# Stick-breaking attention: one head's half of the turned probabilities is copied by VectorE, the other by ScalarE

## The chip, the cores and the metric

The kernel runs on one core of a Trainium2 chip. The metric is the time of one execution on the device in microseconds (us). The core's engines work side by side, each through its own queue in order: TensorE (PE in the profile, with its weight loads as PEld), VectorE (DVE), ScalarE (ACT), GpSimd (POOL) and SyncE (SP), which issues the weight DMAs. They wait for one another through semaphores only.

## What is computed

The program is a whole small model: two blocks of a first network (sparse attention with retention, then stick-breaking attention, each with a convolutional feed-forward part) and one block of a second network. The change lies in the stick-breaking attention, for 16 heads of width 64 over 528 tokens:

```python
def stick_breaking(q, k, v):
    """Strictly causal stick-breaking attention over 128-query blocks. (B,L,H,d) -> (B,L,H,d)."""
    ...
        z = jnp.einsum('bqhd,bkhd->bhqk', q[:, s:e], k[:, :e]).astype(jnp.float32) * scale
        mask = (jnp.arange(e)[None, :] < jnp.arange(s, e)[:, None])[None, None]
        log_1m = jnp.where(mask, jax.nn.log_sigmoid(-z), 0.0)
        rest = lax.cumsum(log_1m, axis=3, reverse=True) - log_1m
        a = jnp.where(mask, jnp.exp(jax.nn.log_sigmoid(z) + rest), 0.0)
        outs.append(jnp.einsum('bhqk,bkhd->bqhd', a.astype(v.dtype), v[:, :e]))
```

The kernel works with products in place of sums of logarithms: a = sigmoid(z) times the running product of sigmoid(-z).

## The kernel before

The order of all work is written out by hand, engine by engine; each stage has one function for each engine. For the stick-breaking stage these are stick_pe, stick_act and stick_dve. The heads are taken in 8 pairs; the 528 queries of a pair are cut into three steps of different width, so there are 24 steps. Step n belongs to pair b = n // 3 and has position x = n % 3. Position 0 has 432 columns a head (three scans a head, of 272, 144 and 16 columns), position 1 has 400, position 2 has 528.

A step passes through these stations:
- stick_z (L1640), TensorE: scores of both heads into two neighbouring PSUM banks, one a head, bank Z_BANK[n % 2] and the next. Signal z_made.
- sigmoids (L1743, L1746), ScalarE: sigmoid(z) into keep, sigmoid(-z) into rest. Signal s_made.
- scans (L1796), VectorE: the running products in rest, head 0, then head 1. Then the multiplication keep times rest (L1807), which makes the probabilities a. Signal a_made.
- stick_turn (L1653, L1656), TensorE: 128x128 blocks of a are turned. Four blocks a head go back into the two banks of the scores (each head has its own bank of 512 columns), odd ones into another bank. Signal a_turned.
- copies (L1762 for the odd blocks, into AX, at two of three positions; L1763 for the 2 x 512 columns of both heads, into AT), ScalarE. Signal a_copied.
- stick_av (L1675), TensorE: product of V with the turned probabilities, into one sum for the pair. It waits for a_copied of its step, and at position 0 also for oT_lo, which says that the pair before has been taken out of PSUM. Signal o_used.
- the pair's result is split into a high part (L1751 on ScalarE, all but four columns; L1754 for those four) and a low part (L1799 and L1803 on VectorE, signals oT_lo and lead_lo).

The stations of different steps are interleaved. In iteration n, TensorE does: filling work, stick_turn of step n-1, filling work, stick_av of step n-1, stick_z of step n+1. The filling work are matmul groups of the projections of later pairs, and at the end of the output projection (L346): four to six groups an iteration up to n = 20, one or two after that, four in n = 24. One projection unit is eight groups; its sum uses one PSUM place, so the next unit starts only when VectorE has taken out the last one (stick_evac, L365 and L367).

ScalarE in iteration n: the sigmoids of step n, a part of a pair's result, then the copies L1762 and L1763 of step n-1, and at positions 0 and 1 (up to pair 7 and pair 6) the split of a weight unit into its high part (L431), after which GpSimd makes the low part (L2574).

VectorE in iteration n: stick_evac at positions 1 and 2 (up to n = 20), the scans of step n, a low part of a result, the multiplication L1807 of step n. It has no copy of turned blocks.

Of the kernel before, what the change touches and what calls it, by code (L numbers as in the profile page):

```python
# [9 lines left out]
ACT = mybir.ActivationFunctionType  # L10
# [155 lines left out]
def program(nc, xT, w_all, params, consts, extra, sinks, relb1, relb2, scratch, out):  # L166
    ctx = ExitStack()
    with ctx:
# [9 lines left out]
        ps = ctx.enter_context(nc.psum_tensor("ps", [P, 8, 512], F32))  # L178
# [43 lines left out]
        class Cut:  # L222
# [39 lines left out]
            "m_std", "mg_sum", "mg_hi", "memset_done", "stage_dve", "o_used", "row_done", "gain_both", "rs_first",  # L262
            "rs_mean", "rs_second", "gate_act", "row_bias", "out_gate", "u_made", "u_read", "mo_exp", "m_sq",
            "e_read", "m_h", "m_hi", "m_y", "m_lo", "ret_t", "ret_sum", "ret_sq", "ret_hi", "ret_y", "ret_lo",
            "mo_den", "mo_done", "m_den", "m_rd", "a_made", "lead_lo", "a_turned", "a_copied", "s_made", "lead_hi",
            "sink_neg", "sel_made", "part_hi", "part_rest", "part_mid", "part_lo")}
        turn_done = [signal(f"turn_done{q}") for q in range(2)]
        turn_out = [signal(f"turn_out{q}") for q in range(2)]
# [1291 lines left out]
        STEPS = 3 * PAIRS  # L1560
# [98 lines left out]
        def stick_av(pe, d, m):  # L1659

            b, x = m // 3, m % 3
            pe.wait_ge(sig["a_copied"].sem, m + 1)
            if x == 0 and b:
                pe.wait_ge(sig["oT_lo"].sem, b)
            for t, tiles in STEP_AV[x]:
                c0, c1 = (0, LEAD) if t < 0 else (LEAD + P * t, LEAD + P * t + P)
                for i, (s, slot) in enumerate(tiles):
                    for hh in range(2):
                        if slot == "e0":
                            a = d["AX"][:, P * hh:P * hh + P]  # L1670
                        elif slot == "e1":
                            a = d["AX"][:, 256 + 124 * hh:256 + 124 * hh + LEAD]
                        else:
                            a = d["AT"][:, hh, P * slot:P * slot + P]
                        mm = pe.matmul(o_sums(slice(64 * hh, 64 * hh + 64), c0, c1),  # L1675
                                       d["V"][:, s, P * b + 64 * hh:P * b + 64 * hh + 64], a,
                                       start=(i == 0), stop=(i == len(tiles) - 1), skip_group_check=True)
            sig["o_used"].by(mm)
# [47 lines left out]
        def stick_act(act):  # L1726
# [8 lines left out]
            for n in range(STEPS + 2):  # L1735
# [19 lines left out]
                if 0 <= n - 1 < STEPS:  # L1755
                    m, bank = n - 1, Z_BANK[(n - 1) % 2]
                    act.wait_ge(sig["a_turned"].sem, m + 1)
                    if m:
                        act.wait_ge(sig["o_used"].sem, m)
                    e = EXTRA_COLS[m % 3]  # L1760
                    if e:
                        act.activation(d["AX"][:, 0:e], ps[:, A_BANK, 0:e], ACT.Copy)  # L1762
                    sig["a_copied"].by(act.activation(d["AT"], ps[:, bank:bank + 2, :], ACT.Copy))  # L1763
                if x == 1 and b + 1 < PAIRS:
                    split_after(act, CQK, (2 * b + 2,))
                if x == 0 and 1 <= b < PAIRS:
# [2 lines left out]
        def stick_evac(v, u):  # L1769
            q_k = stick_qk(u // 2)[u % 2]  # L1770
            woven_evac(v, CQK.first + u, UB, q_k[:, ::-1] if u % 2 else q_k, 1.0 if u % 2 else 64 ** -0.5)

        def stick_dve(v):
            d = stick_views()
# [11 lines left out]
            for n in range(STEPS + 2):  # L1786
# [3 lines left out]
                if n < STEPS:  # L1790
                    w, keep, rest = STEP_WIDTH[x], d["keep"][x], d["rest"][x]
                    v.wait_ge(sig["s_made"].sem, n + 1)
                    for hh in range(2):
                        for at, k, first in STEP_SCANS[x]:
                            r = rest[:, hh * w + at:hh * w + at + k]
                            dve.by(v.tensor_tensor_scan(r, r, d["start"][:, first:first + k], 0.0, ALU.mult, ALU.add))  # L1796
                if x == 1 and n >= 4:
                    v.wait_ge(sig["oT_hi"].sem, b)
                    sig["oT_lo"].by(v.tensor_tensor(rest_cols(Yl, b - 1), o_sums(slice(0, P), LEAD, T3),  # L1799
# [1014 lines left out]
```

## Time and profile before

| what | us |
|---|---|
| median of 3 runs | 2392.09 |
| lowest and highest run | 2391.22, 2392.62 |
| the profiled execution | 2387.57 |
| its span in the profile | 2385.80 |
| TensorE busy | 2348.3 (98%) |
| VectorE busy | 1103.0 (46%) |
| ScalarE busy | 854.6 (36%) |
| GpSimd busy | 919.2 (39%) |

The stick-breaking steps lie between 918 and 1100 us from the start of the span. Times of the profile are counted from there. A row of the timeline names the start, the duration, the engine, the line, the operation and its operands, how many follow one another, and in brackets the idle time of the engine just before, with the instruction that ended it. All of the kernel's arena is in SBUF, ps is PSUM. The granted clock of TensorE was 1.00 throughout the stage.

### The profile page before, as it was taken

The page shows a single profiled execution, that of the slowest core. Times are in us where ns is not written, and L with a number is a line of the kernel's source. Part 1 is how long each engine was busy: PE and PEld are TensorE (multiplying, and loading weights), DVE is VectorE, ACT ScalarE, POOL GpSimd, SP SyncE. Part 2 cuts the span into 40 slices and gives each one's busy share as a digit, 9 for nine tenths or more (in the row PEclk, how much of TensorE's full clock was granted, in tenths as well). Part 3 has the DMA queues.
Part 4 walks back from the last instruction along what each step waited for, and adds up shares of the span by engine and source line. Part 5 has one row for each costly group of instructions (what it writes and reads, how often), then busy time and mean ns, then how long its engine had stood idle before and what let it go on. Part 6 is the DMA issues. An engine that isn't in the chain of part 4 may idle for free.

```text
span 2385.8 us, 37842 instructions
## 1 busy us (share of the span) xinstructions
PE 2348.3 (98%) x15316; PEld 2066.7 (87%) x15316; DVE 1103.0 (46%) x1676; ACT 854.6 (36%) x1320; POOL 919.2 (39%) x382
## 2 busy tenths in 40 slices
PE   7999999999999999999999999999999999999999
PEld 7898999999999999898988888767667888888887
DVE  4885353573442534555644435343473337422222
ACT  4334433332222334554322224454464333322222
POOL 4321223344444442123444444422224455444443
PEclk9999999999999999999999999999999999999999
DMA  5121222222222231111232222322213333323232
GB/s 179 66 72 37 73 65 87 89 88 93 87 103 88 88 107 59 54 54 54 89 105 88 90 104 89 107 72 71 71 54 106 106 106 106 106 88 105 88 106 88
DMA packets 33463, 208.12 MB, mean 87 GB/s; under 512 B 3754, under 2 KB 6420, under 8 KB 9284
## 3 DMA queue, kind: packets, MB, share of 16 engines
q1 hardware_dynamic: 29552, 202.00, 24.7%
q10 hardware_dynamic: 3796, 4.45, 0.6%
q8 instruction: 89, 1.46, 0.3%
q14 instruction: 26, 0.21, 0.0%
HBM read 204.24 MB, written 2.12 MB: 86 GB/s over the span
## 4 chain that ended last, share of the span: by engine, by line
issue 59%; POOL 24%; PE 16%; POOLq 1%; DMA 0%; ACT 0%; DVE 0%; SPq 0%; DVEq 0%; ACTq 0%
POOL wl L2574 24%; PE ps L393 14%; PE ps L346 1%; PE ps L328 1%; POOLq L2573 0%; POOLq L2578 0%; DMA raw<-in_w_all 0%; ACT L431 0%; ACT wh L431 0%; PE ps L489 0%; DVE X L464 0%; SPq L2541 0%; DVEq L464 0%; ACTq L430 0%
## 5 line engine op out<-in xcount | busy, mean ns | idle before, releaser
L2574 POOL TENSOR_TENSOR wl<-raw,wh 128x1024 fp32r<-128x1024 f32 x376 | 918.9, 2448 | 1450.0 <-ACT wh L431 1449.8
L431 ACT ACTIVATE wh<-raw 128x1024 fp32r<-128x1024 f32 x376 | 395.2, 1054 | 758.3 <-PE ps L393 501.5
L393 PE MATMUL ps<-Hh,wl 128*128 128x264 f32 (+2 forms) x1736 | 480.6, 325 | 0.0
L393 PE MATMUL ps<-Hl,wh 128*128 128x264 f32 (+2 forms) x1736 | 480.6, 325 | 0.0
L393 PE MATMUL ps<-Hh,wh 128*128 128x264 f32 (+2 forms) x1736 | 480.5, 325 | 0.0
L393 PEld LDWEIGHTS ps<-Hh,wh 128*128 128x128 f32 x1736 | 291.7, 188 | 28.5 <-issue 0.2
L393 PEld LDWEIGHTS ps<-Hh,wl 128*128 128x128 f32 x1736 | 291.1, 188 | 27.8
L393 PEld LDWEIGHTS ps<-Hl,wh 128*128 128x128 f32 x1736 | 291.1, 188 | 27.4
L346 PE MATMUL ps<-Hh,wh 128*128 128x264 f32 (+1 forms) x1056 | 277.4, 326 | 4.9 <-DVE arena L365 4.0
L346 PE MATMUL ps<-Hl,wh 128*128 128x264 f32 (+1 forms) x1056 | 255.9, 306 | 0.0
L346 PE MATMUL ps<-Hh,wl 128*128 128x264 f32 (+1 forms) x1056 | 255.8, 306 | 0.0
L393 PE MATMUL ps<-Yh,wh 128*128 128x512 f32 (+1 forms) x844 | 251.4, 338 | 0.7 <-DVE Yl L888 0.7
L393 PE MATMUL ps<-Yl,wh 128*128 128x512 f32 (+1 forms) x844 | 251.3, 338 | 0.0
L393 PE MATMUL ps<-Yh,wl 128*128 128x512 f32 (+1 forms) x844 | 251.2, 338 | 0.0
L464 DVE TENSOR_TENSOR X<-ps,X 128x512 f32 (+4 forms) x96 | 67.0, 697 | 328.0 <-PE ps L393 289.9
L346 PEld LDWEIGHTS ps<-Hh,wh 128*128 128x128 f32 x1056 | 171.0, 188 | 43.3 <-issue 31.6
L346 PEld LDWEIGHTS ps<-Hl,wh 128*128 128x128 f32 x1056 | 171.0, 188 | 9.6 <-issue 2.4
L346 PEld LDWEIGHTS ps<-Hh,wl 128*128 128x128 f32 x1056 | 170.8, 188 | 9.6
L393 PEld LDWEIGHTS ps<-Yh,wh 128*128 128x128 f32 x844 | 145.0, 188 | 17.6 <-DVE Yl L888 0.9
L393 PEld LDWEIGHTS ps<-Yl,wh 128*128 128x128 f32 x844 | 144.8, 188 | 16.7
L393 PEld LDWEIGHTS ps<-Yh,wl 128*128 128x128 f32 x844 | 144.7, 188 | 16.7
L642 DVE SCALAR_TENSOR_TENSOR arena<-arena,par 128x528 f32<-128x528 f32 (+1 forms) x44 | 106.9, 2430 | 7.3 <-DVE arena L640 4.1
(255 smaller groups left out, 2810.8 us busy)
## 6 DMA issues: line engine op xcount, KB each, us to landing
raw<-in_w_all SPq DMA_DIRECT2D x188, 1024.0 KB, 4.8
X<-in_xT SPq DMA_DIRECT2D x4, 528.0 KB, 9.3
arena<-scratch ACTq DMA_DIRECT2D x2, 1024.0 KB
arena<-in_extra ACTq DMA_DIRECT2D x2, 528.0 KB
out<-X SPq DMA_DIRECT2D x1, 1024.0 KB, 4.2
out<-X SPq DMA_DIRECT2D x4, 256.0 KB, 2.0
arena<-in_extra ACTq DMA_DIRECT2D x2, 264.0 KB
cst<-in_consts SPq DMA_DIRECT2D x1, 448.0 KB, 11.1
```

Source lines behind the costliest of these rows:

```text
L328: mm = pe.matmul(ps[:, 2 * j + h, 0:c1 - c0], w[:, j, k, :], moving(x, k, c0, c1), start=(k == 0 and part == 0), stop=(k == KB - 1 and par ...
L346: mm = pe.matmul(ps[:, bank + h, 0:c1 - c0], w[:, j, k, :], moving(x_, blk, c0, c1), start=(first and part == 0), stop=(last and part == 2))
L393: mm = pe.matmul(ps[:, 2 * j + h + bank, 0:c1 - c0], w[:, j, k, :], moving(x, blk, c0, c1), start=(at == 0 and part == 0), stop=(at == len ...
L431: act.activation(wh[:, j], raw[:, j // 2, :, P * (j % 2):P * (j % 2) + P], ACT.Copy).then_inc(hi_split, 1)
L464: v.tensor_tensor(x, acc(j, T), x, ALU.add).then_inc(acc_free[j], 1)
L642: dve.by(v.scalar_tensor_tensor(out=c1[:, mm], in0=gs[:, mm, skip + 1:T + 1], scalar=w[mm][1], in1=c1[:, mm], op0=ALU.mult, op1=ALU.add))
L2574: pool.tensor_tensor(wl[:, j], raw[:, j // 2, :, P * (j % 2):P * (j % 2) + P], wh[:, j].bitcast(F32), ALU.subtract).then_inc(split_ready[j ...
```

## The change

ScalarE's copy L1763 takes only head 0 (512 columns of the first bank). Head 1's half, the second bank, is copied by VectorE in a new helper half_copy, with a signal a_half of its own. In iteration n, VectorE does it for step n-1 between the scans of head 0 and the scans of head 1 of step n; for the last step it stands alone in iteration 24. stick_av waits for both signals. half_copy waits for a_turned of its step and for o_used of the one before, the same two for which ScalarE's copy waits.

```diff
@@ stick_av
             pe.wait_ge(sig["a_copied"].sem, m + 1)
+            pe.wait_ge(sig["a_half"].sem, m + 1)
@@ stick_act
-                    sig["a_copied"].by(act.activation(d["AT"], ps[:, bank:bank + 2, :], ACT.Copy))
+                    sig["a_copied"].by(act.activation(d["AT"][:, 0], ps[:, bank, :], ACT.Copy))
@@ new, before stick_dve
+        def half_copy(v, d, m):
+            v.wait_ge(sig["a_turned"].sem, m + 1)
+            if m:
+                v.wait_ge(sig["o_used"].sem, m)
+            sig["a_half"].by(v.tensor_copy(d["AT"][:, 1], ps[:, Z_BANK[m % 2] + 1, :]))
@@ stick_dve, in the loop over n
                     for hh in range(2):
                         for at, k, first in STEP_SCANS[x]:
                             r = rest[:, hh * w + at:hh * w + at + k]
                             dve.by(v.tensor_tensor_scan(r, r, d["start"][:, first:first + k], 0.0, ALU.mult, ALU.add))
+                        if n and hh == 0:
+                            half_copy(v, d, n - 1)
+                if n == STEPS:
+                    half_copy(v, d, n - 1)
```

VectorE's queue in the order of the program, from the scans of a step at position 2 to the scans of the next step at position 0. Before (a scan is printed there as SCALAR_TENSOR_TENSOR):

```order
L1796 SCALAR_TENSOR_TENSOR arena<-arena 128x528 x2
L1803 TENSOR_TENSOR Yl<-ps,Yh 128x4
L1807 TENSOR_TENSOR arena<-arena 128x1056
L1796 SCALAR_TENSOR_TENSOR arena<-arena 128x272
L1796 SCALAR_TENSOR_TENSOR arena<-arena 128x144
L1796 SCALAR_TENSOR_TENSOR arena<-arena 128x16
L1796 SCALAR_TENSOR_TENSOR arena<-arena 128x272
L1796 SCALAR_TENSOR_TENSOR arena<-arena 128x144
L1796 SCALAR_TENSOR_TENSOR arena<-arena 128x16
L1807 TENSOR_TENSOR arena<-arena 128x864
```

After, the same place (L1803 is now the scan, L1814 and L1818 are the old L1803 and L1807):

```order
L1803 SCALAR_TENSOR_TENSOR arena<-arena 128x528
L1778 COPY arena<-ps 128x512
L1803 SCALAR_TENSOR_TENSOR arena<-arena 128x528
L1814 TENSOR_TENSOR Yl<-ps,Yh 128x4
L1818 TENSOR_TENSOR arena<-arena 128x1056
L1803 SCALAR_TENSOR_TENSOR arena<-arena 128x272
L1803 SCALAR_TENSOR_TENSOR arena<-arena 128x144
L1803 SCALAR_TENSOR_TENSOR arena<-arena 128x16
L1778 COPY arena<-ps 128x512
L1803 SCALAR_TENSOR_TENSOR arena<-arena 128x272
L1803 SCALAR_TENSOR_TENSOR arena<-arena 128x144
L1803 SCALAR_TENSOR_TENSOR arena<-arena 128x16
```

A copy stands between the heads of each step, so head 1's scans and the multiplication come behind it.

TensorE's queue at the first product with V, with the semaphores that it waits for. Before:

```order
L346 MATMUL ps<-Hh,wh 128x264 x2
L346 MATMUL ps<-Hl,wh 128x264 x2
L346 MATMUL ps<-Hh,wl 128x264 x2
L1675 MATMUL ps<-arena 64x128 [waits a_copied]
L1675 MATMUL ps<-arena 64x128 x9
```

After:

```order
L346 MATMUL ps<-Hh,wh 128x264 x2
L346 MATMUL ps<-Hl,wh 128x264 x2
L346 MATMUL ps<-Hh,wl 128x264 x2
L1676 MATMUL ps<-arena 64x128 [waits a_half,a_copied]
L1676 MATMUL ps<-arena 64x128 x9
```

Nothing changes place on TensorE; one wait is added to each product.

## Rows read from the trace of the kernel before

**Rows 1.** Busy us by stretch: PE, PEld, DVE, ACT, POOL, then clock, DMA.
```profile
967.00:1075.00 108.00, 107.80 (x1013) 97.02 (x1013) 55.45 (x80) 54.86 (x82) 24.05 (x10) 1.00 0.15 50
1075.00:1093.00 18.00, 14.61 (x149) 12.53 (x146) 9.60 (x16) 10.46 (x16) 2.92 (x1) 1.00 0.00 1
```

**Rows 2.** Groups by form: line, engine, operation, shape, count | busy us, mean ns.
```profile
L1763 ACT ACTIVATE arena<-ps 128x1024 f32<-128x1024 f32 x24 | 24.6, 1025 | 13.8 <-PE ps L1656 13.8
...
L735 ACT ACTIVATE arena<-ps 128x512 f32<-128x512 f32 x4 | 2.4, 600 | 4.7 <-PE ps L695 4.7
...
L1796 DVE TENSOR_TENSOR_SCAN arena<-arena 128x528 f32<-128x528 f32 x16 | 19.2, 1241 | 3.7 <-ACT arena L1743 3.7
...
L737 DVE TENSOR_SCALAR arena<-ps 128x512 f32<-128x512 f32 x6 | 4.2, 692 | 7.5 <-PE ps L695 7.5
...
L1141 DVE COPY arena<-ps 64x528 f32<-64x528 f32 x1 | 0.7, 711 | 2.7 <-PE ps L1031 2.7
```

**Rows 3.** Timeline (start, us, what), a regular iteration at position 2.
```profile
959.05 2.40 DVE L1796 TENSOR_TENSOR_SCAN arena<-arena 128x528 f32<-128x528 f32 x2
...
960.90 0.86 PEld L1675 LDWEIGHTS ps<-arena 128*64 128x64 f32 x16
```

**Rows 4.** Timeline, a regular iteration at position 0 and the next turning.
```profile
942.33 2.21 DVE L1796 TENSOR_TENSOR_SCAN arena<-arena 128x272 f32<-128x272 f32 x6 [2.05 <-ACT arena L1743]
...
943.64 1.02 ACT L1763 ACTIVATE arena<-ps 128x1024 f32<-128x1024 f32 x1
...
944.57 1.06 DVE L1807 TENSOR_TENSOR arena<-arena 128x864 f32<-128x864 f32 x1
...
944.71 1.08 PEld L1675 LDWEIGHTS ps<-arena 128*64 128x64 f32 x20
...
945.68 2.37 POOL L2574 TENSOR_TENSOR wl<-raw,wh 128x1024 fp32r<-128x1024 f32 x1 [13.32 <-ACT wh L431]
...
948.41 0.47 PEld L1653 LDWEIGHTS ps<-cst,arena 128*128 128x128 f32 x4
...
950.03 0.49 ACT L1762 ACTIVATE arena<-ps 128x384 f32<-128x384 f32 x1 [0.70 <-PE ps L1656]
```

**Rows 5.** Timeline, the last iterations n = 21, 22 and 23, by engine.
```profile
1077.24 2.21 DVE L1796 TENSOR_TENSOR_SCAN arena<-arena 128x272 f32<-128x272 f32 x6 [2.15 <-ACT arena L1743]
1083.04 1.88 DVE L1796 TENSOR_TENSOR_SCAN arena<-arena 128x400 f32<-128x400 f32 x2 [2.50 <-ACT arena L1746]
1084.83 0.67 DVE L1799 TENSOR_TENSOR Yl<-ps,Yh 128x512 fp32r<-128x512 f32 x1
1090.10 2.41 DVE L1796 TENSOR_TENSOR_SCAN arena<-arena 128x528 f32<-128x528 f32 x2 [3.71 <-ACT arena L1743]
...
1079.85 2.92 POOL L2574 TENSOR_TENSOR wl<-raw,wh 128x1024 fp32r<-128x1024 f32 x1 [12.61 <-ACT wh L431]
...
1078.88 1.09 PEld L1675 LDWEIGHTS ps<-arena 128*64 128x64 f32 x20 [0.88 <-ACT arena L1763]
...
1081.86 0.46 PEld L1653 LDWEIGHTS ps<-cst,arena 128*128 128x128 f32 x4
...
1085.61 1.32 PEld L1675 LDWEIGHTS ps<-arena 128*64 128x64 f32 x24 [1.66 <-ACT arena L1763]
...
1091.10 0.86 PEld L1675 LDWEIGHTS ps<-arena 128*64 128x64 f32 x16 [1.47 <-ACT arena L1763]
```

**Rows 6.** Timeline, two places elsewhere where VectorE and GpSimd overlap.
```profile
456.99 2.29 DVE L548 SCALAR_TENSOR_TENSOR Hl<-X,par,Hh 128x528 fp32r<-128x528 f32 x1
459.20 2.90 DVE L554 TENSOR_TENSOR arena<-arena 128x528 f32<-128x528 f32 x1
...
458.87 2.66 POOL L2574 TENSOR_TENSOR wl<-raw,wh 128x1024 fp32r<-128x1024 f32 x1 [0.16 <-ACT wh L431]
...
1571.06 2.36 POOL L2574 TENSOR_TENSOR wl<-raw,wh 128x1024 fp32r<-128x1024 f32 x1 [15.56 <-ACT wh L431]
...
1571.49 3.01 DVE L2114 TENSOR_TENSOR_SCAN arena<-arena 4x512 f32<-4x512 f32 x1
```

More of the change, by code:

```diff
@@ L264, in program @@
             "e_read", "m_h", "m_hi", "m_y", "m_lo", "ret_t", "ret_sum", "ret_sq", "ret_hi", "ret_y", "ret_lo",
-            "mo_den", "mo_done", "m_den", "m_rd", "a_made", "lead_lo", "a_turned", "a_copied", "s_made", "lead_hi",
+            "mo_den", "mo_done", "m_den", "m_rd", "a_made", "lead_lo", "a_turned", "a_copied", "a_half", "s_made", "lead_hi",
             "sink_neg", "sel_made", "part_hi", "part_rest", "part_mid", "part_lo")}
```

## The prediction

> **What bounds the kernel now.** I read first the busy time by stretch, to see whether TensorE has any room in the stick-breaking stage, then TensorE's weight loads in order of time, to see what its few gaps wait for, and last the same seconds on VectorE, ScalarE and GpSimd. TensorE is the bound: in the regular part of the stage it is busy 107.80 of 108.00 us, so a copy made shorter on another engine gives nothing there. In the last steps it is busy 14.61 of 18.00 us, because the filling work has thinned out to one group of matmuls at a time [rows 1]. There it waits three times before the product with V (L1675): 0.88 us, 1.66 us and 1.47 us [rows 5]. The profile puts all three on ScalarE's copy L1763. The first and the third are that: step 20's copy starts long after the turned blocks are there, and the product follows its end. The second is not: this product also needs the low part of the pair before, L1799 on VectorE, which starts at 1084.83, takes 0.67 and ends at 1085.50; the product starts at 1085.61. So from VectorE's end to TensorE's start I count 0.11 us.
>
> **What one half costs on either engine.** ScalarE's copy falls from 128x1024, 1.025 us, to 128x512; the nearest row is L735 with 0.600 us [rows 2]. So ScalarE is free 0.43 us earlier, 24 times. VectorE gets 24 copies of 128x512 out of PSUM. The nearest rows are L737, a TENSOR_SCALAR of that shape from PSUM, 0.692 us, and L1141, a real COPY from PSUM, 0.711 us for 528 columns and 64 partitions; I take 0.69 us. Bounds are 0.60 (as fast as ScalarE) and 0.71. Two instructions in a row on VectorE overlap by some 0.08: two scans of 1.241 us take 2.40 together, a stride of 1.16. So what follows a copy is moved by about 0.61, I take 0.60.
> The Trainium skill (VectorE: DVE Perf Modes, section on the TRN2 errata) prices a copy from PSUM on VectorE at 120 cycles plus one a column at 0.96 GHz, an estimate of 0.66 us for 512 columns. By it every term below in which the copy's end counts would be 0.03 smaller, 0.2 in the whole sum; the measured rows decide.
>
> **The regular steps.** A step has position x = n mod 3. *x = 2* (seven steps, n = 2 to 20): the scan of head 0 starts at 959.05, the copy can start 1.16 later at 960.21, ends at 960.90, and TensorE can go on at 961.01. Before, the product started at 960.90 [rows 3]. That is 0.11 us later, for the six steps n = 2 to 17. The seventh, n = 20, I leave out: its filling work is already the output projection's, with a start of its own. **Six times 0.11 = 0.66 us.** With a copy of 0.60 it would be near 0.1, with 0.71 it is 0.8.
> *x = 0*: the scans start at 942.33; two heads and the start of the multiplication lie 2.24 apart, so one head takes about 1.08. The copy runs from 943.41 to 944.10 and TensorE may start at 944.21; it starts at 944.71 anyway. Nothing lost. The multiplication L1807 moves from 944.57 to 945.17 and would end at 946.23; the turning that needs it starts at 948.41 [rows 4]. Nothing lost either, unless GpSimd gets in between (a rival below).
> *x = 1*: ScalarE shows the turned blocks ready at 950.03 [rows 4]; the copy is done within 1 us of that, and four groups of filling matmuls stand between the turning and the product, so it is hidden. The evacuations L365 and L367, on which TensorE's next unit waits, stand ahead of the scans in VectorE's order and are not touched. The extra wait on TensorE I take at nothing: products with one and with two waits start alike.
>
> **The last steps**, where nothing hides a wait [rows 5].
> *n = 21 (x = 0)*, product of step 20: scans start at 1077.24, the copy at 1078.32, it ends at 1079.01; TensorE goes on at 1079.11 where it did at 1078.88: **+0.23**. ScalarE's half is ready 0.4 earlier, but now VectorE's comes last.
> Then GpSimd. ScalarE's weight split stands right behind its copy and moves 0.43 earlier, and with it GpSimd's L2574, from 1079.85 to 1079.42. VectorE's scans of head 1 have been moved to 1078.92 to 1080.08 and stand in the way. What happens then, other places show [rows 6]: GpSimd's instruction came at 458.87 while VectorE ran L548; as L548 ended, at 459.28, GpSimd went first, and VectorE's next instruction took 2.90 us, until 0.57 after GpSimd's end. A scan does the same: it took 3.01 us beside GpSimd's 2.36. So I expect that GpSimd takes over when the scan of 272 columns ends (1079.64) and runs about 2.25 us, to 1081.89; the rest of the scans ends near 1082.2, the multiplication runs from 1082.31 to 1083.37, and the turning of step 21 starts at 1083.48. Without GpSimd it would start at 1081.86 + 0.23 = 1082.09.
> *n = 22 (x = 1)*: the turned blocks are there 1.62 later (948.41 to 950.03 in [rows 4]), at 1085.10. VectorE, done with head 0's scan by 1084.2, stands waiting for them; copy to 1085.79, head 1's scan from 1085.70, L1799 from 1086.59 to 1087.26, product at 1087.37 where it was 1085.61: **+1.76 in all so far** (0.23 + 0.60 = 0.83 if GpSimd did not come in between: the copy alone moves L1799 by 0.60).
> *n = 23 (x = 2)*: the scans start at 1090.10 after ScalarE, so they only move with the rest. Copy from 1091.26 to 1091.95, product at 1092.06 instead of 1091.10: **+0.96**. The last copy (n = 24) has four groups to hide behind.
> Sum for the last steps: 1.76 + 0.96 = **2.72 us**; with 0.66 from the regular steps **3.4 us longer**. It adds to TensorE's stream, which has no gap behind the stage that could take it up. The profiled execution took 2387.57 us (span 2385.80), 4.5 under the median of the runs, 2392.09; the 3.4 us are the same in both. **Forecast: 2395.5 us**, plus 0.14%.
>
> **The rivals.**
> *A. GpSimd does not get in between in n = 21.* Then the last steps cost 0.23 + 0.60 + 0.96 = 1.79 and the whole 2.45: 2394.5 us. For it: no row shows a takeover between two scans of one run, and they follow each other without a gap. Against it: the takeover at 458.87 was between two instructions without a gap as well. Chance 0.25.
> The Trainium skill (SBUF — State Buffer, section on who interferes with whom) says that VectorE's instructions with two SBUF inputs and GpSimd's that read SBUF exclude each other for a whole instruction, and that a VectorE instruction with at most one SBUF input does not contend. The rows on L554 and the scan agree; by the same rule the added copy, which reads PSUM, is itself never held up, and B and C below hang on the moved instructions alone.
> *B. Slower by more than 0.2%: GpSimd gets in ahead of the multiplication in the regular x = 0 steps.* GpSimd's split moves from 945.68 to 945.25, the multiplication from 944.57 to 945.17 [rows 4]: VectorE is ahead by 0.08, where it was ahead by 1.1. If the copy or its wait costs 0.1 more than I take, GpSimd goes first, to 947.62; the multiplication (0.57 behind it for 0.70 us, so 0.93 for its 1.06) ends at 948.55, and the turning starts at 948.66 instead of 948.41. That is 0.25 for each of six steps, 1.5 us: 2397.0 us, just past the 0.2%. It decides from 0.1 us on, and both moved times are estimates; but the copy's 0.69 is well shown and its blocks are ready in time. Chance 0.2.
> *C. Faster, or no loss: the halves really run side by side.* If VectorE's half were ready with ScalarE's, the products at 1078.88 and 1091.10 would come 0.4 earlier each, and 2391.3 us is the least I can reach. Against it: VectorE's scans start after ScalarE's sigmoids in every step, and the copy stands behind one head of them; in n = 23 ScalarE's own copy would be done before VectorE's starts. Chance 0.05. A gain over 0.2% would need 4.8 us, more than all three waits together.
>
> **How the numbers follow.** Forecast 0.5, A 0.25, B 0.2, C 0.05. A measurement of this kernel tells 0.2%, 4.8 us, from no change. The forecast, A and C are within it; B lies on its edge, and a stall that I have missed would come on top. So faster 0.03, same 0.77, slower 0.20. The range takes in A with a copy of 0.60 us and half of C below, 2392.0, and above B with a copy of 0.71 us and 1 us for what the waits themselves cost, 2398.5.
>
> **What would show it.** In the profile after: 24 rows of COPY from PSUM near 0.69 us, 24 of ScalarE's copy near 0.60; in the regular x = 2 steps a product that starts 0.1 later behind VectorE's copy; in the last steps TensorE waiting for VectorE at three products, with about 2.7 us more idle time between 1075 and 1096, and a scan or multiplication on VectorE of over 2 us at n = 21. Wrong it would be if that scan is not held up (A), if L1807's successor in regular x = 0 steps takes 3 us (B), if the copies take over 0.8 us or wait for the turned blocks in every step, or if TensorE shows new gaps at the evacuations.

## The result, and the profile after

| | before | changed |
|---|---|---|
| median, us | 2390.85 (2387.92 to 2392.71, 22 runs) | 2395.08 (2391.25 to 2396.05, 22 runs) |
| the profiled execution, us | 2387.57 | 2391.54 |
| its span, us | 2385.8 | 2389.7 |

The changed kernel takes 1.0016 times as long, with an interval of 1.0010 to 1.0022: about 3.8 us more (2.4 to 5.3). The 0.2% that were set as the bound of "no change" are 4.8 us; the ratio is within it, and only the upper end of its interval is past it. The medians themselves are 4.2 us apart, the lowest runs 3.3. Forecast were 3.4 us more and 2395.5 us. The two profiled executions are 3.97 us apart.

The 22 times of either kernel stand in two clusters: before, 9 at 2387.9 to 2388.5, 11 at 2391.2 to 2392.7 and 2 between; changed, 5 at 2391.3 to 2391.7 and 17 at 2393.9 to 2396.1. The profiled execution of either kernel lies at its lower cluster. One execution of a later kernel (regular steps only) took 6447.61 us and is left out of that kernel's ratio.

The busy time by stretch stands first, as in [rows 1]. Columns are the stretch, its length, busy us of PE, PEld, DVE, ACT and POOL with the number of instructions, then granted clock and DMA share.

```profile
967.00:1075.00 108.00, 107.58 (x1005) 96.90 (x1005) 73.25 (x95) 49.25 (x82) 27.93 (x10) 1.00 0.14 50
1075.00:1093.00 18.00, 14.17 (x141) 11.83 (x136) 12.05 (x17) 8.77 (x16) 2.35 (x1) 1.00 0.00 1
1094.00:1100.00 6.00, 5.11 (x37) 4.81 (x38) 3.20 (x5) 0.00 (x0) 0.00 (x0) 0.72 0.00 0
```

In the regular part TensorE is still busy nearly throughout. VectorE has grown from 55.45 to 73.25 us and ScalarE has shrunk from 54.86 to 49.25, and neither matters to TensorE there. VectorE's growth is more than its 15 added instructions: about half of it is a wait, shown below at position 1. The last line is new: a granted clock of 0.72 over 6 us in the last steps, where it was 1.00 before. 6 x 0.28 = 1.7 us of TensorE's time is lost at half clock (1.2 GHz in place of 2.4).

The two halves, groups by form, answer to [rows 2]:

```profile
L1778 DVE COPY arena<-ps 128x512 f32<-128x512 f32 x24 | 16.1, 670 | 4.5 <-PE ps L1656 4.5
L1764 ACT ACTIVATE arena<-ps 128x512 f32<-128x512 f32 x24 | 14.3, 596 | 13.7 <-PE ps L1656 13.7
```

A regular iteration at position 2, VectorE and then TensorE's weight load, answers to [rows 3]:

```profile
959.72 1.25 DVE L1803 TENSOR_TENSOR_SCAN arena<-arena 128x528 f32<-128x528 f32 x1
960.88 0.67 DVE L1778 COPY arena<-ps 128x512 f32<-128x512 f32 x1
...
961.66 0.89 PEld L1676 LDWEIGHTS ps<-arena 128*64 128x64 f32 x16 [0.24 <-issue]
```

The copy ends at 961.55 and the product starts 0.11 later, 1.94 us behind the first scan where it was 1.85 before. A regular iteration at position 0 answers to [rows 4]:

```profile
943.00 1.16 DVE L1803 TENSOR_TENSOR_SCAN arena<-arena 128x272 f32<-128x272 f32 x3 [1.58 <-ACT arena L1744]
944.08 0.67 DVE L1778 COPY arena<-ps 128x512 f32<-128x512 f32 x1
...
945.84 1.06 DVE L1818 TENSOR_TENSOR arena<-arena 128x864 f32<-128x864 f32 x1
...
945.92 3.21 POOL L2585 TENSOR_TENSOR wl<-raw,wh 128x1024 fp32r<-128x1024 f32 x1 [12.80 <-ACT wh L431]
```

The multiplication is 0.08 us ahead of GpSimd, as worked out, and keeps its 1.06 us; GpSimd pays, with 3.21 in place of 2.37, and nobody waits for it. One position on, at position 1, VectorE and GpSimd:

```profile
952.98 2.96 DVE L1818 TENSOR_TENSOR arena<-arena 128x800 f32<-128x800 f32 x1
...
952.71 2.37 POOL L2585 TENSOR_TENSOR wl<-raw,wh 128x1024 fp32r<-128x1024 f32 x1 [3.58 <-ACT wh L431]
```

and VectorE in the kernel before:

```profile
951.71 0.98 DVE L1807 TENSOR_TENSOR arena<-arena 128x800 f32<-128x800 f32 x1
```

In the changed kernel GpSimd is 0.27 us ahead, and the multiplication takes 2.96 us where it took 0.98 before. The same stands in each of the six regular steps at position 1. The prediction looked at position 0 only. It costs TensorE nothing: the multiplication ends at 955.94, and the turning that needs it starts at 958.79.

The last iterations answer to [rows 5]; VectorE, GpSimd, then TensorE's weight loads:

```profile
1078.47 1.16 DVE L1803 TENSOR_TENSOR_SCAN arena<-arena 128x272 f32<-128x272 f32 x3 [1.57 <-ACT arena L1744]
1079.54 0.67 DVE L1778 COPY arena<-ps 128x512 f32<-128x512 f32 x1
1080.12 3.28 DVE L1803 TENSOR_TENSOR_SCAN arena<-arena 128x272 f32<-128x272 f32 x3
1083.44 1.06 DVE L1818 TENSOR_TENSOR arena<-arena 128x864 f32<-128x864 f32 x1
...
1086.12 0.69 DVE L1778 COPY arena<-ps 128x512 f32<-128x512 f32 x1 [0.63 <-PE ps L1656]
...
1087.63 0.67 DVE L1810 TENSOR_TENSOR Yl<-ps,Yh 128x512 fp32r<-128x512 f32 x1
...
1094.08 0.67 DVE L1778 COPY arena<-ps 128x512 f32<-128x512 f32 x1
...
1080.66 2.35 POOL L2585 TENSOR_TENSOR wl<-raw,wh 128x1024 fp32r<-128x1024 f32 x1 [12.70 <-ACT wh L431]
...
1080.32 1.11 PEld L1676 LDWEIGHTS ps<-arena 128*64 128x64 f32 x20 [1.09 <-ACT arena L1764]
1084.56 0.42 PEld L1653 LDWEIGHTS ps<-cst,arena 128*128 128x128 f32 x4 [1.18 <-DVE arena L1818]
1088.41 1.33 PEld L1676 LDWEIGHTS ps<-arena 128*64 128x64 f32 x24 [1.81 <-issue]
1094.86 1.34 PEld L1676 LDWEIGHTS ps<-arena 128*64 128x64 f32 x16 [2.42 <-issue]
...
1103.79 1.09 PEld L1676 LDWEIGHTS ps<-arena 128*64 128x64 f32 x20
```

This is the forecast of n = 21: GpSimd comes in at 1080.66, between the scans of head 1, which take 3.28 us in place of 1.16. The multiplication is late, and TensorE gets a wait it did not have (1.18 us before the turning, L1653). At 1094.86 the weight loads of a product take 1.34 us where the same 16 took 0.86 before: that is the half clock.

Two of the brackets say "issue", and the first names ScalarE's copy, although VectorE's ended last (1080.21, and 0.11 later TensorE). With two semaphores to wait for, the bracket says little; the end of the last of the awaited instructions says it.

**Where the time went.** A distance between two products with V is free of whatever shifted the kernel earlier. The product of step n - 1 stands in iteration n. In us, from the starts of L1675 (before) and L1676 (after):

| from one product to the next | before | changed | more |
|---|---|---|---|
| a whole pair in the regular part (three steps) | 22.47 | 22.58 | 0.11, for six pairs 0.67 |
| step 19 to 20 | 5.54 | 5.76 | 0.22 |
| step 20 to 21 | 6.73 | 8.09 | 1.36 |
| step 21 to 22 | 5.49 | 6.45 | 0.96 |
| step 22 to 23 | 7.37 | 8.93 | 1.56 |

Together 4.8 us in the stage. The first four lines, 3.2 us, are the forecast's terms; the last is the clock, which it did not have. In front of the stage the changed kernel's profile is 0.5 us late already (first weight load of L793 that waits: 25.44 before, 25.89 after). Behind the stage it gets time back: before had half clock near 1575 us, in the second network, and after had not.

```profile
1572.00:1578.00 6.00, 6.00 (x21) 4.41 (x20) 3.08 (x2) 3.34 (x3) 3.07 (x2) 0.72 0.53 175
```

That is before; the changed kernel has 1.00 at this place. So the difference of the two profiled executions, 3.97, is not the forecast's sum come true: it is 3.2 of it, 1.6 of clock more and about as much less elsewhere, 0.5 of start-up, and some 0.3 that none of these account for. How much of that belongs to the change and how much to the execution is what the experiments had to tell.

### The profile page after: what moved, and what is told of

It reads as the page before. It is cut to its first block, busy times and chain, and to the rows that moved or that the text cites. A ratio compares the mean times of both kernels' runs of the same rounds, so it can differ in the third digit from the quotient of the medians.

```text
span 2389.7 us, 37906 instructions
## 1 busy us (share of the span) xinstructions
PE 2349.2 (98%) x15316; PEld 2067.2 (87%) x15316; DVE 1132.3 (47%) x1700; ACT 845.0 (35%) x1320; POOL 925.1 (39%) x382
## 3 DMA queue, kind: packets, MB, share of 16 engines
HBM read 204.24 MB, written 2.12 MB: 86 GB/s over the span
## 4 chain that ended last, share of the span: by engine, by line
issue 59%; POOL 24%; PE 16%; POOLq 1%; DMA 0%; ACT 0%; DVE 0%; SPq 0%; DVEq 0%; ACTq 0%
POOL wl L2585 24%; PE ps L393 14%; PE ps L346 1%; PE ps L328 1%; POOLq L2584 0%; POOLq L2589 0%; DMA raw<-in_w_all 0%; ACT L431 0%; ACT wh L431 0%; PE ps L489 0%; DVE X L464 0%; SPq L2552 0%; DVEq L464 0%; ACTq L430 0%
## 5 line engine op out<-in xcount | busy, mean ns | idle before, releaser
L431 ACT ACTIVATE wh<-raw 128x1024 fp32r<-128x1024 f32 x376 | 395.4, 1055 | 756.2 <-PE ps L393 498.8
```

The costliest lines, as they stand in the source:

```text
L431: act.activation(wh[:, j], raw[:, j // 2, :, P * (j % 2):P * (j % 2) + P], ACT.Copy).then_inc(hi_split, 1)
```

## The experiments

The theory was that the sum of the forecast is right and that the rest is a property of the execution, the clock falling behind the longer waits. The rival was that the change costs something else too, for instance the second wait on TensorE or the moved multiplications. So the kernels are read by the distance table, and the timing decides only where it can. All their lines are moved against the changed kernel's by one to four.

**Each of the two once more.** No edit: one more profile of the kernel before and of the changed one.

> The kernel before, unchanged, for a second trace of it. TensorE's product of step 22 at the same distance from the scans of step 23 as in the first trace (1.00 us), three waits of 0.9, 1.7 and 1.5 us in the last steps and full clock there. If the lower clock after the stage (near 1573 us in the first trace) belongs to the kernel, it is there again; if it comes and goes, it is not.

> The changed kernel, unchanged, for a second trace. Theory 1 (the waits in the last steps lower the clock): the wait before the product of step 22 is again about 2.4 us, and TensorE again runs at half clock for 3.4 us right behind it, which costs about 1.6 us. Theory 2 (the clock falls at some place of its own choosing): the half clock is elsewhere or nowhere, and the last steps cost 1.6 us less than in the first trace. The regular steps lose 0.11 us a pair by both.

The distances came back to within 0.02 us: 22.47, 5.54, 6.72, 5.50, 7.36 for the kernel before and 22.58, 5.78, 8.08, 6.45, 8.95 for the changed one. The fall of the clock in the last steps was there again in the changed kernel,

```profile
1090.00:1102.00 12.00, 9.79 (x77) 8.47 (x73) 4.77 (x6) 2.97 (x6) 0.00 (x0) 0.86 0.00 0
```

and the one near 1575 us was absent again. The kernel before had it twice as long there (12 x 0.28 = 3.4 us lost), and another one near 188 us.

```profile
188.00:192.00 4.00, 3.50 (x18) 3.53 (x19) 2.07 (x9) 1.12 (x4) 0.00 (x0) 0.59 0.82 266
1572.00:1584.00 12.00, 10.18 (x30) 7.75 (x31) 5.15 (x5) 5.26 (x7) 4.75 (x2) 0.72 0.25 87
```

So the distances belong to the kernel, and half clock comes and goes in units of 1.7 us between executions of one kernel. The two executions of the kernel before lost 1.7 and 5.1 us to it, which is 3.4 of the 3.7 us between their times. That the spread of its other runs (2387.92 to 2392.71) has the same cause is likely and not shown.

**The halves in the last steps only, and in the regular steps only.** Both start from the changed kernel. For the last steps only:

```diff
@@ stick_av
-            pe.wait_ge(sig["a_half"].sem, m + 1)
+            if m >= 20:
+                pe.wait_ge(sig["a_half"].sem, m - 19)
@@ stick_act
+                    if m >= 20:
                         sig["a_copied"].by(act.activation(d["AT"][:, 0], ps[:, bank, :], ACT.Copy))
+                    else:
+                        sig["a_copied"].by(act.activation(d["AT"], ps[:, bank:bank + 2, :], ACT.Copy))
@@ stick_dve
-                        if n and hh == 0:
+                        if n > 20 and hh == 0:
```

> Halves only for steps 20 to 23, ScalarE's full copy for the 20 steps before. My theory: the regular steps lose nothing, the last ones 2.5 to 2.9 us by waits (0.2 + 1.3 + 1.0), and about 1.6 more if the clock falls there. The rival, that the loss is spread over all steps: most of the 3.4 us is gone.

The other kernel, regular steps only, has `m < 20` for both conditions, the wait on a_half against m + 1, and half_copy for n = 1 to 20 only.

> Halves only for steps 0 to 19, ScalarE's full copy for steps 20 to 23. My theory: 0.11 us for each of six pairs, 0.7 us in all, no takeover by GpSimd at the end, the last steps as before. The rival: more than 1.5 us, if the copies cost TensorE something in every step.

| | regular pair | 19 to 20 | 20 to 21 | 21 to 22 | 22 to 23 | median | ratio |
|---|---|---|---|---|---|---|---|
| last steps only | 22.47 | 5.75 | 8.08 | 6.46 | 8.89 | 2393.75 | 1.0014 (1.0004 to 1.0024) |
| regular steps only | 22.58 | 5.55 | 6.73 | 5.49 | 7.37 | 2390.73 | 1.0001 (0.9992 to 1.0011) |

The parts are the changed kernel's to 0.04 us and do not touch one another. Last steps alone are slower by a margin that the timing can tell; the regular steps' 0.67 us it cannot. TensorE waits for a second semaphore 20 times in the second kernel and only the 0.11 a pair shows, which is the copy's end at position 2. The second wait as such costs nothing that can be seen.

**GpSimd's share in n = 21.** The last weight split before GpSimd's work (L431, at x = 0 of the last pair) is put behind the stage:

```diff
@@ stick_act
-                if x == 0 and 1 <= b < PAIRS:
+                if x == 0 and 1 <= b < PAIRS - 1:
                     ...
+                if n == STEPS:
+                    split_after(act, CQK, (2 * PAIRS - 1,))
```

> The changed kernel, but ScalarE's last weight split of the stage (unit 15, in n = 21) stands behind its copies of n = 24, so GpSimd has no work while VectorE does steps 21 and 22. If GpSimd's takeover caused part of the loss: head 1's scans in n = 21 take 1.16 us instead of 3.28, no wait before the turning of step 21, and the product of step 21 starts 0.75 to 0.9 us earlier against that of step 20. If the copy alone did it, nothing changes. If it is the amount of waiting that lowers the clock, the half clock may go as well, another 1.6 us; if only the last wait of 2.4 us counts, it stays.

VectorE and TensorE's weight loads of that kernel:

```profile
1082.69 1.15 DVE L1805 TENSOR_TENSOR_SCAN arena<-arena 128x272 f32<-128x272 f32 x3
...
1085.89 0.47 PEld L1653 LDWEIGHTS ps<-cst,arena 128*128 128x128 f32 x4
...
1090.23 2.45 PEld L1676 LDWEIGHTS ps<-arena 128*64 128x64 f32 x24 [2.25 <-issue]
```

The scans of head 1 take 1.15 again, the turning no longer waits, and step 20 to 21 falls from 8.09 to 7.34: GpSimd's share is 0.75 us, and the copy's own 0.61 remain (7.34 - 6.73). But the clock fell earlier, at this product (24 loads in 2.45 us, not 1.33), and 21 to 22 took 8.05, then 22 to 23 only 7.40. The time, 2393.53 us, is 1.0011 (1.0002 to 1.0021) times that of before. So taking away GpSimd takes away its 0.75, but in this execution not the fall of the clock. The 1.6 us of the clock (8.05 - 6.45) came one product earlier instead, behind a wait of 2.25 us.

**The copy of step 22 back on ScalarE.**

```diff
@@ stick_av
-            pe.wait_ge(sig["a_half"].sem, m + 1)
+            if m != 22:
+                pe.wait_ge(sig["a_half"].sem, m + 1 - (m > 22))
@@ stick_act
+                    if m != 22:
                         sig["a_copied"].by(act.activation(d["AT"][:, 0], ps[:, bank, :], ACT.Copy))
+                    else:
+                        sig["a_copied"].by(act.activation(d["AT"], ps[:, bank:bank + 2, :], ACT.Copy))
@@ stick_dve
-                        if n and hh == 0:
+                        if n and n != 23 and hh == 0:
```

> The changed kernel, but the copy of step 22 is ScalarE's alone, as before; 23 halves are left. The product of step 22 should start 0.96 us earlier against the scans of step 23. If the long wait there lowers the clock, the half clock goes too and the last steps are 2.5 us shorter in all; if the waits of n = 21 and 22 do it, only 0.96.

```profile
1091.58 1.32 PEld L1677 LDWEIGHTS ps<-arena 128*64 128x64 f32 x24 [1.81 <-issue]
1097.07 0.86 PEld L1677 LDWEIGHTS ps<-arena 128*64 128x64 f32 x16 [1.47 <-ACT arena L1768]
```

21 to 22 is back at 5.49, 22 to 23 at 7.37, and the wait is the 1.47 of [rows 5] again. The clock stayed at 1.00 in the last steps; this is one trace, and the kernels below keep 1.00 there with the long wait too, so it does not show that the shorter wait is the reason. The 0.96 are this one copy, as forecast. Median 2390.84, ratio 1.0004 (0.9995 to 1.0014).

**Is GpSimd ahead of the multiplication (rival B)?** In the changed kernel the margin is 0.08 us. A fill of unused columns ahead of the multiplication uses it up:

```diff
@@ stick_dve, ahead of the multiplication
+                if x == 0 and 0 < n < 21:
+                    v.memset(arena[:, 13000:13192], 0.0)
```

> The changed kernel with one memset of 192 unused columns (about 0.2 us) on VectorE ahead of the multiplication in the regular steps at position 0 (n = 3 to 18). In the changed kernel the multiplication starts 0.08 us ahead of GpSimd. My theory: GpSimd now goes first, the multiplication takes 3.2 us instead of 1.06, GpSimd 2.37 instead of 3.21, the turning behind it starts 0.25 us later, 1.4 us over six steps. The rival, that only the order of the queues counts: 0.2 us more of VectorE's time with over 2 us to spare, nothing on TensorE.

Both instructions began in the same moment, and VectorE was first: the multiplication took 1.00 us.

```profile
948.12 1.00 DVE L1820 TENSOR_TENSOR arena<-arena 128x864 f32<-128x864 f32 x1
...
948.12 3.23 POOL L2587 TENSOR_TENSOR wl<-raw,wh 128x1024 fp32r<-128x1024 f32 x1 [12.79 <-ACT wh L431]
```

The fill had taken 0.22 us only. A longer one (columns 13000 to 13448) was to make it clear.

> As pool_first, with a memset of 448 unused columns in place of 192. The small one moved the multiplication by only 0.12 us, and it still started together with GpSimd and went first. This one should move it by 0.38, so that GpSimd comes first by 0.3 us. My theory: the multiplication takes over 3 us, GpSimd 2.37, and the turning behind it starts 0.2 to 0.3 us later in each of six steps, 1.2 to 1.8 us in all. The rival: nothing on TensorE, since two microseconds are to spare.

```profile
947.23 0.43 DVE L1817 MEMSET arena<- 128x448 f32 x1
947.58 0.99 DVE L1820 TENSOR_TENSOR arena<-arena 128x864 f32<-128x864 f32 x1
...
954.37 2.96 DVE L1820 TENSOR_TENSOR arena<-arena 128x800 f32<-128x800 f32 x1
...
947.31 3.50 POOL L2587 TENSOR_TENSOR wl<-raw,wh 128x1024 fp32r<-128x1024 f32 x1 [12.78 <-ACT wh L431]
...
954.10 2.37 POOL L2587 TENSOR_TENSOR wl<-raw,wh 128x1024 fp32r<-128x1024 f32 x1 [3.29 <-ACT wh L431]
```

GpSimd's row now begins 0.27 us ahead of the multiplication's, and still VectorE goes first, and GpSimd takes 3.50. At position 1 of the same trace, as in the changed kernel, GpSimd's row is ahead by the same 0.27, and the multiplication takes 2.96: there it waits. What differs is what stands ahead of it on VectorE, the fill in one place and L1810, which reads PSUM, in the other. It may be that the fill itself holds GpSimd off; that was not tried apart. In both kernels a regular pair stays at 22.58. Rival B was not made to happen in this way, and where its edge lies is not told. In the changed kernel itself it did not happen at any of the regular x = 0 steps: the multiplication takes 1.06 us in each.

Both kernels are of use for the clock. Their last steps have the changed kernel's waits to 0.02 us (5.77, 8.09, 6.44 and 5.76, 8.09, 6.45), and 22 to 23 takes 7.40 in both, with 1.00 granted:

```profile
1097.05 0.89 PEld L1676 LDWEIGHTS ps<-arena 128*64 128x64 f32 x16 [2.42 <-issue]
...
1090.00:1102.00 12.00, 9.15 (x91) 8.03 (x92) 6.01 (x8) 2.82 (x6) 0.00 (x0) 1.00 0.01 1
```

That is the short fill. The same 2.42 us of waiting, and no fall. Their medians are 2395.08 and 2394.48 us, ratios 1.0012 (1.0003 to 1.0022) and 1.0013 (1.0004 to 1.0023).

**The copy ahead of the scans.** VectorE copies first and scans behind it:

```diff
@@ stick_dve
+                if 0 < n <= STEPS:
+                    half_copy(v, d, n - 1)
                 ...
-                        if n and hh == 0:
-                            half_copy(v, d, n - 1)
-                if n == STEPS:
-                    half_copy(v, d, n - 1)
```

> The changed kernel with VectorE's copy of step n-1 ahead of all scans of step n, not between the heads. In regular steps at position 2 the product should lose nothing now (the turned blocks are there 0.25 us after the scans could start, and the copy ends 0.9 us before the product is due). At position 0 VectorE waits 1.0 us for the turned blocks, its scans and multiplication move by 1.6 us, and GpSimd gets in between: the turning behind them 0.9 us later in each of six steps. In the last steps the products of steps 20 and 22 come 0.4 us earlier than before the change, that of step 21 later. If the place alone was at fault, the whole is faster than the changed kernel; my theory says slower, by 4 to 6 us.

```profile
946.75 4.32 DVE L1805 TENSOR_TENSOR_SCAN arena<-arena 128x272 f32<-128x272 f32 x6
951.10 1.06 DVE L1816 TENSOR_TENSOR arena<-arena 128x864 f32<-128x864 f32 x1
...
948.04 2.63 POOL L2583 TENSOR_TENSOR wl<-raw,wh 128x1024 fp32r<-128x1024 f32 x1 [13.06 <-ACT wh L431]
...
952.21 0.42 PEld L1653 LDWEIGHTS ps<-cst,arena 128*128 128x128 f32 x4 [0.95 <-DVE arena L1816]
...
956.17 0.66 DVE L1808 TENSOR_TENSOR Yl<-ps,Yh 128x512 fp32r<-128x512 f32 x1
...
956.95 1.33 PEld L1676 LDWEIGHTS ps<-arena 128*64 128x64 f32 x24 [0.51 <-issue]
```

2402.60 us, ratio 1.0051 (1.0035 to 1.0068): 7.5 us more than the changed kernel's median, where 4 to 6 were expected. The six scans take 4.32 us in place of 2.21 in every regular x = 0 step, since GpSimd comes in among them; the turning waits 0.95 us for it, and a pair takes 23.82, 1.35 more than before. I had put that at 0.9: what I had left out is the low part L1808, which now ends at 956.83 and makes the next product wait 0.51. The gain that was expected is there too, 19 to 20 in 5.11 in place of 5.54, but 20 to 21 takes 9.88. So the cost that rival B described is real: VectorE's work of an x = 0 step, broken into by GpSimd, makes the turning late. The change's order just avoids it.

**Is the second wait VectorE's?** In [rows 5] the profile puts the wait before the product of step 21 on ScalarE's copy; the prediction said it was L1799, the low part of the pair's result. This kernel is the one before with L1799 between the scans of the two heads:

```diff
@@ stick_dve, in the kernel before
+                        if x == 1 and n >= 4 and hh == 0:
+                            low_part(v, b)
-                if x == 1 and n >= 4:
+                if x == 1 and n > STEPS:
                     ...
```

low_part is L1799 with its wait for oT_hi and its signal oT_lo, as a helper.

> The kernel before with one move: the low part L1799 stands between the scans of the two heads at position 1, and no half is copied by VectorE. My theory: in n = 22 the product of step 21 waited for L1799, not for ScalarE's copy as the profile puts it; it now waits for the copy alone and starts 0.68 us earlier; the regular steps stay as they are. The rival, that the profile's releaser is right: no change.

```profile
1084.42 0.67 DVE L1775 TENSOR_TENSOR Yl<-ps,Yh 128x512 fp32r<-128x512 f32 x1
...
1085.40 1.30 PEld L1675 LDWEIGHTS ps<-arena 128*64 128x64 f32 x24 [0.98 <-ACT arena L1763]
```

20 to 21 takes 6.04 in place of 6.73: 0.69 less for 0.68 expected. Nothing was done to ScalarE, so the bracket in [rows 5] named the wrong engine. The wait that is left, 0.98, may really be ScalarE's. The time, 2389.21 us, ratio 0.9995 (0.9986 to 1.0004), is not told from before.

**What of it could be kept.** VectorE takes its half only for step 20, and ahead of the scans; the low part stands between the heads; the last split is late.

```diff
@@ stick_av
-            pe.wait_ge(sig["a_half"].sem, m + 1)
+            if m == 20:
+                pe.wait_ge(sig["a_half"].sem, 1)
@@ stick_act
+                    if m == 20:
                         sig["a_copied"].by(act.activation(d["AT"][:, 0], ps[:, bank, :], ACT.Copy))
+                    else:
+                        sig["a_copied"].by(act.activation(d["AT"], ps[:, bank:bank + 2, :], ACT.Copy))
@@ stick_dve, ahead of the scans
+                if n == 21:
+                    half_copy(v, d, 20)
```

The calls of half_copy between the scans and in iteration 24 are gone; the moves of the low part and of the split are those shown above and are left out here.

> early_low, and besides in the last steps only: VectorE copies head 1's half of step 20 ahead of the scans of step 21, and the last weight split stands behind the copies of n = 24. Expected against the kernel before: product of step 20 0.4 us earlier, product of step 21 another 0.7 to 1.0, regular steps unchanged, so 1.1 to 1.4 us in all (0.05%), less than the timing can tell. A loss would come if VectorE's later multiplication of step 21 is late for its turning (0.1 us by my count).

```profile
1080.76 1.08 PEld L1677 LDWEIGHTS ps<-arena 128*64 128x64 f32 x20 [0.45 <-ACT arena L1766]
1086.81 1.30 PEld L1677 LDWEIGHTS ps<-arena 128*64 128x64 f32 x24 [0.97 <-ACT arena L1768]
```

19 to 20 in 5.12 (0.42 less) and 20 to 21 in 6.05 (0.68 less), 1.1 us in all; the first wait of [rows 5] falls from 0.88 to 0.45. In the time, 2388.89 us against 2390.41, ratio 0.9995 (0.9986 to 1.0004), it is no more than a hint. Of the places tried this is the one where splitting the copy pays: a wait of TensorE for ScalarE's copy, and VectorE idle at that moment.

**What remains when start-up and clock are taken off.** For each profiled execution: the time, the start of L793's weight load behind its wait (start-up, chance of the execution), and the time lost at reduced clock from 100 us to 2380 us, which is the length of each stretch of 4 us times (1 - granted clock), summed.

| kernel | time | start-up | lost to the clock | rest | places of half clock |
|---|---|---|---|---|---|
| before | 2387.57 | 25.44 | 1.7 | 2360.4 | 1575 |
| before, again | 2391.29 | 26.06 | 5.1 | 2360.1 | 188, 1575 twice |
| low part early | 2387.39 | 25.72 | 1.7 | 2360.0 | 1575 |
| kept parts | 2388.70 | 26.14 | 3.4 | 2359.2 | 188, 1575 |
| regular steps only | 2389.01 | 26.08 | 1.7 | 2361.2 | 188 |
| last steps only | 2393.97 | 26.00 | 5.1 | 2362.9 | 1096, 1580 twice |
| step 22 on ScalarE | 2393.62 | 27.15 | 3.4 | 2363.1 | 188, 1580 |
| late split | 2393.40 | 26.70 | 3.4 | 2363.3 | 188, 1092 |
| long fill | 2394.42 | 26.11 | 5.0 | 2363.3 | 188, 1580 twice |
| short fill | 2395.15 | 26.44 | 5.1 | 2363.6 | 188, 1580 twice |
| changed | 2391.54 | 25.89 | 1.7 | 2363.9 | 1096 |
| changed, again | 2392.00 | 26.00 | 1.7 | 2364.3 | 1096 |
| copy ahead of the scans | 2402.82 | 26.54 | 5.2 | 2371.1 | 188, 1100, 1588 |

Without start-up and clock, two executions of one kernel agree to 0.4 us, where their times differ by up to 3.7. The changed kernel's rest is 3.8 above before's (2364.1 to 2360.3, means of two), the regular steps' 1.0 and the last steps' 2.6. By the distances 3.2, 0.7 and 2.5 were due. The 0.6 us between 3.8 and 3.2 have no row of their own. The start-up is read at one point only, and the two fills, which have the same distances, come to 3.2 (2363.45). The late split and step 22 on ScalarE are 3.0 and 2.8 above before where their distances give 2.5 and 2.25. So a rest of a single trace is good to about half a us, and no better.

## Why the prediction was right

- **The bound.** TensorE, with room only in the last steps: right. 3.2 of the 4.8 us in the stage lie at the three waits and the six regular steps that it named. The one new wait of TensorE, 1.18 us before the turning of step 21, is the late multiplication that it had forecast.
- **Price of a half.** The copy took 0.670 us for 0.69, ScalarE's 0.596 for 0.600. The Trainium skill (VectorE: DVE Perf Modes, section on the TRN2 errata) gives an estimate of 0.66; the measured 0.670 is nearer to that than to the row of L737 (0.692) that I went by.
- **Regular steps.** 0.66 forecast, 0.67 measured, 0.11 in each pair and all of it at position 2. Positions 0 and 1 cost nothing, and the evacuations were not touched. The extra wait was taken as nothing, and the kernel with only the regular steps shows no more.
- **n = 21, the copy.** +0.23 forecast, +0.22 measured.
- **n = 21 and 22, GpSimd.** 1.53 forecast, 1.36 measured. GpSimd came between the scans as said. The turning came 4.24 us behind the product of step 20, where 4.37 were forecast, and the product of step 21 3.85 behind the turning, where it was 3.89. GpSimd's share was 0.75 by the late split, where 1.76 - 0.83 = 0.93 had been forecast; the copy's own share 0.61 where it was 0.60. So the takeover was priced 0.18 too high. Part of it is small change: the forecast left 0.11 us between the last scan and the multiplication, which in fact followed at once (1083.40 and 1083.44), and 0.11 from its end to the turning, which came after 0.06.
- **n = 23.** +0.96 both.
- **Sum.** 3.4 forecast, 3.2 measured in distances, about 3.8 in the times. That the times come this close is in part luck: the clock had no term.
- **The clock: the step that was missing.** The rows of the kernel before [rows 1] show a granted clock of 1.00 in the last steps, and the prediction has no term for it. In both traces of the changed kernel a wait of 2.42 us is followed by half clock, which cost 1.56 us before the next product. In these two executions the forecast was saved by half clock that was missing near 1575 us, where the kernel before had it; in both fills, by the same wait having no fall behind it. Both traces of the changed kernel (2391.54 and 2392.00 us) lie at its lower cluster; where the 17 executions of the upper one ran at half clock no trace shows. The term should have stood in the sum as 0 or 1.6, and the range, which ended at 2398.5, held it.
- **The rivals.** A fell: the scans of n = 21 took 3.28 us. B did not happen where it was looked for, at position 0, with the margin of 0.08 us that was worked out; the edge turned out less sharp than I took it. What B describes did happen at position 1, in all six regular steps (2.96 us for 0.98), and cost nothing since 2.8 us were to spare before the turning: the prediction called position 1 hidden without looking at the multiplication there, so that part was right by luck. C did not happen: at all three late products VectorE ended last, with its half at steps 20 and 22 and with the low part behind its half at step 21 (1088.30, the product 0.11 later). The Trainium skill (SBUF — State Buffer, section on who interferes with whom) has the added copy itself never held up, since it reads PSUM: the trace agrees, 24 copies in 16.1 us, 0.67 to 0.69 us each. Its "Issue order, not op shape, decides who blocks" is not so plainly borne out: with the fill ahead, GpSimd's row was 0.27 us early and it still went second. What decides there is open.
- **The direction.** Of 24 halves that VectorE took over, 21 were hidden or came to 0.11, and three were on the path. The gain for ScalarE's copy (0.43 us, 24 times) was real and had no taker, because VectorE's scans start only behind ScalarE's sigmoids, and so its half can't be early there.

## What to carry to other kernels

Splitting a copy over two engines shortens it only if the second engine is idle when the data is there; look at what stands ahead of it in that engine's queue, and at what is moved behind it. An engine that gets free earlier (here ScalarE, and through it GpSimd) starts its next work earlier, and that can hold up somebody's critical work in the middle, as GpSimd's split did to the scans (3.28 us for 1.16): price that as a term of its own, at every place where the two now meet. For a difference of a few us, compare distances between like instructions in the traces, and take start-up and clock off before believing a total.

## What the hardware showed that I had not expected

- Half clock comes in units of 1.7 us of lost time, at places that have a wait ahead of them, but not each time: near 1575 us one or two of them in the kernel before and none in the changed one, behind waits of 2.10 and 2.12 us, and in the last steps, with waits that agree to 0.02 us, once there and once not. In the kernels whose last waits are short (before, low part early, kept parts, regular steps only, step 22 on ScalarE) no trace has it there. What chooses was not settled, but the traces' clock rows give a lead. In both traces of the changed kernel and in last steps only, the clock fell 1075.2 us after it had first risen at the start of the kernel, and that was 0.37, 0.08 and 1.17 us behind the start of step 22's product: the wait of 2.42 us was over. In the two fills the same moment lies some 0.2 and 0.4 us ahead of that product, still inside the wait, and the clock did not fall. In the late split it fell 0.03 us behind the start of a product that had waited 2.25 us. So it may be how the clock's time lies to the kernel's, which the start-up shifts from execution to execution; no run varied it on purpose. The runs of each kernel spread over some 4 us, which is as much as the change costs. The Trainium skill (TensorE: Matmul & The Clock Gate, Part 1 on the clock gate) says of the slow matmuls at a kernel's start that their number varies from run to run; these traces show the like in mid-kernel.
- A run of scans with no gap between them can be broken into by GpSimd: 3.28 us for three that take 1.16, 4.32 for six that take 2.21.
- A fill of 448 columns ahead of the multiplication let VectorE go first although GpSimd's row began 0.27 us before it (0.99 and 3.50 us), where the same distance behind an instruction that reads PSUM went the other way (2.96 and 2.37). The order in which two rows start did not tell which of the two instructions waited.
- An idle bracket names one releaser. Where the instruction waits for two, it named the wrong one in at least two places (the product of step 21 before, that of step 20 after).
